# Rests of nine weight units in the state-space stage: an accumulating transfer in place of VectorE's subtraction

## What is computed

```python
zxbcdt = rms_norm(x, ln_g) @ in_w                 # 1024 x 5152
z, xbc, dt = split(zxbcdt)
xbc = silu(causal_dwconv(xbc, conv_w, conv_b))    # 24 tiles of 128 features
y = ssd_chunked(xs * dt, a, bm, cm) + xs * d_skip # 4 groups, 4 chunks of 128
y = rms_norm(y * silu(z), norm_g)                 # by group
x = x + y @ out_w
```

## The kernel before, in words

| unit | tile | TensorE's ticks |
|---|---|---|
| 9 | ("in", 1, 0) | 29 to 32 |
| 10 | ("in", 1, 1) | 33 to 36 |
| 11 | ("in", 1, 2) | 37 to 40 |
| 12 | ("in", 1, 3) | 41 to 44 |
| 13 | ("in", 1, 4) | 45 to 48 |
| 14 | ("in", 1, 5) | 49 to 52 |
| 26, 27, 28 | ("in", 2, 3), ("in", 2, 4), ("in", 2, 5) | 97 to 108 |

## Time and profile before

### The profile page before, as it was taken

One profiled execution on the slowest core, in us unless ns is written; L12 is line 12 of the kernel. 1 busy time (PEld: TensorE's weight loads), 2 busy tenths in 40 slices (PEclk: granted clock), 3 DMA queues, 4 the chain that ended last, 5 costly groups with the idle time before them and its releaser, 6 DMA issues.

```text
span 2400.7 us, 29668 instructions
## 1 busy us (share of the span) xinstructions
PE 2376.7 (99%) x11556; PEld 1930.8 (80%) x11556; DVE 1403.3 (58%) x2203; ACT 1052.5 (44%) x1803; POOL 370.8 (15%) x297
## 2 busy tenths in 40 slices
PE   8999999999999999999999999999999999999999
PEld 6777888888888877788888877787788877888887
DVE  6778776763665678766456557534555445443343
ACT  6654564442444677644234334324443334322223
POOL 0352252210111000121012100001211001110011
PEclk9999999999999999999999999999999999999999
DMA  4632223223223221232332332231243322223222
GB/s 164 110 92 79 81 74 101 88 86 109 96 82 127 72 71 54 75 102 94 98 102 87 99 131 72 78 102 61 68 132 128 114 97 88 88 95 99 105 78 90
DMA packets 74844, 226.19 MB, mean 94 GB/s; under 512 B 8144, under 2 KB 12368, under 8 KB 74576
## 3 DMA queue, kind: packets, MB, share of 16 engines
q1 hardware_dynamic: 70272, 215.90, 27.5%
q10 hardware_dynamic: 4432, 8.39, 2.0%
HBM read 215.87 MB, written 8.39 MB: 93 GB/s over the span
## 4 chain that ended last, share of the span: by engine, by line
PE 62%; DVE 1%; issue 0%; ACT 0%; POOLq 0%; POOL 0%; DVEq 0%
PE bank L1189 60%; PE bank L1193 1%; DVE t L2073 0%; ACT t L1595 0%; DVE t L2070 0%; DVE t L2081 0%; DVE t L2077 0%; ACT t L1598 0%; DVE t L2563 0%; POOLq L2862 0%; POOL t L2641 0%; DVEq L2862 0%; DVE t L2409 0%; DVE t L2078 0%; DVE t L2569 0%
## 5 line engine op out<-in xcount | busy, mean ns | idle before, releaser
L1189 PE MATMUL bank<-t 128*128 128x512 f32 (+4 forms) x11130 | 2352.3, 377 | 16.7 <-DVE t L2073 7.8
L1189 PEld LDWEIGHTS bank<-t 128*128 128x128 f32 (+2 forms) x11130 | 1888.0, 185 | 450.2 <-issue 80.0
L1595 ACT ACTIVATE t<-t 128x1024 fp32r<-128x1024 f32 (+6 forms) x634 | 539.3, 861 | 645.4 <-PE bank L1189 276.1
L2070 DVE TENSOR_TENSOR t<-t 128x1024 fp32r<-128x1024 f32 (+6 forms) x686 | 624.1, 920 | 260.6 <-ACT t L1595 254.5
L2641 POOL TENSOR_TENSOR t<-t 128x512 f32<-128x512 f32 (+4 forms) x217 | 329.0, 1523 | 1543.9 <-ACT t L1598 558.7
L1598 ACT ACTIVATE t<-t 128x512 f32<-128x512 f32 (+6 forms) x610 | 367.4, 616 | 450.3 <-DVE t L2070 301.2
L2070 DVE TENSOR_TENSOR t<-bank,t 128x512 f32<-128x512 f32 (+4 forms) x412 | 276.0, 674 | 451.9 <-PE bank L1189 441.5
L2073 DVE SCALAR_TENSOR_TENSOR t<-t 128x512 f32<-128x512 f32 (+4 forms) x493 | 364.0, 748 | 103.4 <-ACT t L1598 63.8
L1595 ACT ACTIVATE t<-bank 128x512 f32<-128x512 f32 (+4 forms) x151 | 72.2, 498 | 167.0 <-PE bank L1193 145.2
L2644 POOL TENSOR_SCALAR t<-t 128x128 f32<-128x128 f32 (+3 forms) x64 | 41.1, 649 | 476.8 <-ACT t L1595 246.1
L2073 DVE SCALAR_TENSOR_TENSOR t<-bank,t 128x512 f32<-128x512 f32 x56 | 38.5, 687 | 67.3 <-PE bank L1189 67.3
(11 more groups left out here) (30 smaller groups left out, 52.9 us busy)
## 6 DMA issues: line engine op xcount, KB each, us to landing
t<-in_w SPq DMA_DIRECT2D x304, 512.0 KB, 3.3
t<-in_w SPq DMA_DIRECT2D x48, 384.0 KB, 3.0
t<-in_w SPq DMA_DIRECT2D x56, 320.0 KB, 2.9
t<-in_w SPq DMA_DIRECT2D x28, 256.0 KB, 2.7
tab<-t ACTq DMA_DIRECT2D x1, 2560.0 KB
t<-in_x SPq DMA_DIRECT2D x8, 256.0 KB, 5.3
t<-tab SPq DMA_DIRECT2D x8, 256.0 KB, 3.9
spill<-t ACTq DMA_DIRECT2D x1, 2048.0 KB, 8.7
```

Of the source, the lines that this page charges most:

```text
L1189: return eng.matmul(out, lhs, rhs, start=start, stop=stop, skip_group_check=loose)
L1595: return eng.activation(out, in_, ACT.Copy, scale=scale)
L2070: return eng.tensor_tensor(out, a, b, o)
```

## The change

The nine units make their rest in another way. ScalarE writes minus the rounded part into the rest's buffer (a second copy, with scale -1, right after the first), and GpSimd then issues a transfer from the raw buffer to the rest's buffer that adds to what stands there. The rest's landing is counted on three new semaphores, one for each buffer. TensorE, and SyncE's load of unit u + 3, wait for that landing instead of `cut`. GpSimd issues at the end of the tick in which ScalarE rounds. VectorE skips these units.

```diff
+ADDED_RESTS = tuple((1, i) for i in range(6)) + tuple((2, i) for i in range(3, 6))
...
+                    if key[0] == "in" and key[1:] in ADDED_RESTS:
+                        self.added.add(u)
...
+        self.rest = [Dma(sem(f"rest{i}")) for i in range(N_W)]
...
+    def cut_done(self, u):
+
+        if u in self.plan.added:
+            return self.sig.rest[u % N_W].at(sum(v % N_W == u % N_W for v in self.plan.added if v <= u))
+        return self.sig["cut"].at(u)
...
-        w.wait_ge(*sig["cut"].at(u))
+        w.wait_ge(*K.cut_done(u))
...
         copy(buf.his[u % N_W][:, 0:n], buf.raws[u % N_W][:, 0:n]).then_inc(*sig["cut_hi"].up(u))
+        if u in plan.added:
+            copy(buf.los[u % N_W][:, 0:n], buf.raws[u % N_W][:, 0:n], -1.0).then_inc(*sig["minus_hi"].up(u))
...
         for u in plan.cut_at.get(T, ()):
-            if u < len(plan.units):
+            if u < len(plan.units) and u not in plan.added:
                 cut(u)
...
+    def add_raw(u):
+        n = K.offsets[u][1]
+        w.wait_ge(*sig["minus_hi"].at(u))
+        eng.dma_start(buf.los[u % N_W][:, 0:n].bitcast(F), buf.raws[u % N_W][:, 0:n], accum_op=ADD).then_inc(
+            *sig.rest[u % N_W].up())
...
         end(T)
+        for u in plan.split_at.get(T - 1, ()):
+            if u in plan.added:
+                add_raw(u)
...
         if u >= N_W:
-            w.wait_ge(*sig["cut"].at(u - N_W))
+            w.wait_ge(*K.cut_done(u - N_W))
```

More of the change, by code:

```diff
@@ L160, in __init__ @@
         self.pieces = []
-        self.units, self.unit_end = [], {}
+        self.units, self.unit_end, self.added = [], {}, set()
         self.split_at, self.cut_at, self.split_n, self.cut_age = {}, {}, 0, 2
@@ L799 @@
 SIGNALS = (
-    "cut_hi", "cut", "unit",
+    "cut_hi", "minus_hi", "cut", "unit",
     "halves", "mhalf", "identb", "identr", "maskb",
```

## The result

The changed kernel takes 2432.81 us (median; 2429.03 to 2435.24) against 2402.56 before: ratio 1.0120, 95 % interval 1.0102 to 1.0138, 30.3 us slower where +11.4 was forecast. That lies inside the range given (2398 to 2438); the sign and the place were right, the size was not.

A forecast was written before the change was run, and what follows sets the result against it. The prediction took TensorE to bound the kernel, busy 2376.7 of 2400.7 us. Its terms, 9 + 2.5 + 6 + 1.6 - 6.7 - 1.0 = +11.4 us, laid on the median 2402.56, gave 2414, range 2398 to 2438.

The forecast's parts named there:

- the wait at 192: TensorE's 1.33 us wait for VectorE before 192.59; its possible return was set against unit 27's 1.1 us lateness, nothing in sum.
- A: Rival, 13 %: the transfers are slow in themselves, 10 us in the quiet, so units 9, 10, 27 and 28 miss too; 2427.
- B: Rival, 19 %: the rests pass the table store, unit 12 lands at 71, only small relief of -1 to -2.3 us remains; 2401.
- C: Rival, 8 %: queue turns beside the store are short, 3.5 to 6.5 us; loss nearly all given back, 0 to +5; 2404.
- D: Rival, 10 %: unit 14's load overtakes the store if unit 11's rest lands by 58.5; -7 us likely, 2395.5.
- I let the rest land with it, at 80.5: Unit 12's rest, beside the table store, lands with the held weight loads; TensorE waits 9 us plus 2.5 us of clock.
- The weight loads' train: Weight loads issued at 60.1, 68.2 and 73.7, taken as held by the store until some 75, landing at 79.7, 83.6 and 87.5.
- Unit 13 ... lands with the same train. Nothing: Unit 13's rest lands with the held weight loads, before TensorE has done unit 12 at 90; no cost.
- Unit 14, with 6 forecast: Unit 14's rest lands at 103.8, TensorE waits 7.6 us plus 2.5 of clock; taken at six tenths, 6 us.
- The waits absorb the old one ... 6.7 us come back, and 1.0 us: New TensorE waits swallow the one before 96.51: 4.2 + 2.5 = 6.7 us come back, plus 1.0 of VectorE's backlog.
- the signs named beforehand: TensorE's longest wait ends at 79 to 82, wait at 96.5 gone, loads 15 and 16 late, nine subtractions fewer, nine copies more.
- the old wait: TensorE's 4.17 us wait before 96.51 in the kernel before, put down to unit 14's late raw weights, with 2.5 us of clock.

The follow-up runs named there:

- probe_copy: Kernel before plus two plain 448 KB transfers that nobody in the stage waits for, at the places of unit 9's and unit 12's rests; 2404.89 us, one run.
- probe_add: Kernel before plus two adding 448 KB transfers that nobody in the stage waits for, at the places of unit 9's and unit 12's rests; 2406.2 us, one run.
- without_12: Changed kernel with unit 12 alone given back to VectorE; 2422.63 us, ratio 1.0079 to the kernel before.
- small_store_after: Changed kernel with both table stores cut to a sixteenth of their rows (attention biases left wrong); 2399.91 us, ratio 0.9981 to the kernel before.
- no_rests: Changed kernel with all nine rests left out (no negative copy, transfer or subtraction; result lacks them); 2395.13 us, ratio 0.9965 to the kernel before.
- only_12: Changed kernel with only unit 12's rest made by transfer, the other eight back on VectorE; 2424.19 us, ratio 1.0084 to the kernel before.
- pool_near: Changed kernel with GpSimd subtracting for units 12 to 14, the other six rests by transfer; 2402.89 us, ratio 0.9996 to the kernel before.
- no_rests_near: Changed kernel with rests of units 12 to 14 left out, the other six back on VectorE; 2398.50 us, ratio 0.9979 to the kernel before.

## Why the prediction was wrong

**Right**: TensorE bounds; the loss is where the table store runs. In the quiet a rest lands in 4.5 to 5.3 us (I took 5), its issue costs GpSimd 0.86 to 1.06 us (I took 1), the clock behind unit 12's stop costs 2.7 (I took 2.5), units 9 to 11 and 26 to 28 cost nothing, the wait at 192 is given back, and unit 12 is the first to stop TensorE. Of the rivals, A, B, C and D all fell: quiet rests are short, those beside the store neither passed it nor got a short turn, and unit 14's load came after the store, since unit 11's rest landed at 61.5 and not by 58.5. B was right for half of a transfer's packets and wrong for the half that decides. The rule that I had weighed in C (the Trainium skill, DMA: Bandwidth & Descriptors, section Queues, rings and completion order: the engines change queues after some 9 to 17 descriptors) gave, as I used it, a turn of 3.5 to 6.5 us; the held half of probe_copy stood for 10.7. The estimate of 3.2 us for 512 KB in the quiet that I worked out from the Trainium skill (DMA: Bandwidth & Descriptors, section Anatomy of one DMA) fits a plain transfer (3.2 measured for 448 KB), but not an adding one (4.5 to 5.3 for 512 KB).

**The step that failed first** is "I let the rest land with it, at 80.5". It landed at 89.6. The weight loads' train was the right neighbour for a plain transfer (84.3 in probe_copy), 4 us later than I had put it; an adding one needs 5 to 7 us more (89.6 here, 90.9 in probe_add). So the term for unit 12, 9 + 2.5 = 11.5, measured 20.6: 9.1 of the 18.9 us between forecast (+11.4) and result (+30.3).

**Second**, "Unit 13 ... lands with the same train. Nothing": its rest took 31.0 us behind unit 12's on the same queue, and cost 7.0. There was no train to land with: from 84.2, when unit 14's load landed, to 89.6 no load was in flight, and the rest landed at 102.8. Unit 12's rest in front is only a part of it, since alone in without_12 it took 22.1.

Unit 14, with 6 forecast, measured 6.4, and that is luck. I had its rest issued at 83 and landing at 103.8, against TensorE at 96.2: 10.1 us of wait and clock, of which I took six tenths. It was issued at 86.5 and landed at 116.7, against TensorE at 113.1: the landing moved by 13 us and TensorE by 17.

**Third**, "The waits absorb the old one ... 6.7 us come back, and 1.0 us": only 2.2 did, and 1.6 at unit 27. I had shifted TensorE in the sum and left ScalarE where it was. But the load of unit 15 hangs on unit 12's rest and that of 16 on 13's; I had given this chain 1.6 us, and it held ScalarE 16.35 us at 100 to 117. From 103 to 113 VectorE stood too, so this was not VectorE's backlog, and the exponentials were as late as TensorE was. Of this step the forecast was -6.7 - 1.0 + 1.6 = -6.1 and the measured shift -2.2 - 1.6 = -3.8, so 2.3 us less came back. In all 9.1 + 7.0 + 0.4 + 2.3 = 18.8 of the 18.9 us.

Of the signs named beforehand, the counts of subtractions and copies and the late loads (units 15 and 16 at 89.6 and 102.8, "80 and later") came true; the long wait ends at 89.75 instead of 79 to 82, and the old wait is not gone but shorter.

**The cause of the old wait** was wrong as well, though it cost the sum little. I put 4.17 us to unit 14's late raw weights. The runs show VectorE's backlog. With it I priced the relief, the very thing that the change is for, at 1 to 2.3 us (rival B) where it is worth 8.1. With the rests not held the change wins, 2399.91 in small_store_after; even there a wait of 1.89 us for ScalarE is left before 94.4, against 1.22 in no_rests.

What stays open is why the second half of a transfer waits so long beside a store that, by the stretches, leaves a third or more of the engines' time unused (DMA share 0.64 from 70 to 95, 0.57 from 103 to 113). The traces show that half of the packets pass and half are held; they do not name the engine of a packet, nor what ends the hold.

## To carry to other kernels

A transfer that takes over an engine's work must be priced by the busiest stretch it falls in, not by the median: list every transfer that is in flight then, and let yours land after the last of those, with its own slow packets on top. If a buffer's next load hangs on it, shift the engines that feed on that load too before counting on slack given back. And take the cause of a wait from an experiment that moves the suspected producer alone; a producer that was late need not be the one that was waited for.

## What was not expected of the hardware

- Beside the 2.5 MB store, half of a transfer's packets pass at once and half are held: 40 of 80 by 67.3 and none until 78.0 (probe_copy), 72 of 144 by 70.0 and none until 78.7 (only_12).
- An adding transfer from SBUF to SBUF takes the DMA engines 2.2 times as long as a plain one of the same 448 KB (10.0 against 4.5 % of their time from 40 to 100): 6.0 against 3.2 us in the quiet, 26.4 against 19.4 beside a 2.5 MB store.
- Issuing a second large store 1.3 us behind the first on the same queue held ScalarE for 19.02 us. It is not that the first is still running: in the kernel before the second is issued 36.7 us behind it, some 19 us before the first ends, and the issue took 0.67 us.
- A subtraction of 128x1024 takes GpSimd 2.4 to 2.8 us and stretches VectorE's neighbouring operation on two operands from 0.75 to 2.3 and 2.8 us.
- The length of an idle stretch of TensorE does not by itself tell the clock behind it. After 1.87 us (pool_near, before 70.24) and 2.24 us (only_12, before 120.55) the granted clock was 1.00 over the next 5 us; after 1.88 us (no_rests_near, before 92.93) it was 0.66 over 93 to 98; after 4.2 us it was 0.50 for 5 us, and after 17.9 us it was 0.50 for 5 us as well.
